# Stick-breaking attention: the second head's multiply moves from VectorE to GpSimd, with a third tail buffer

## The chip, the cores and the metric

The kernel runs on one core of a Trainium2 chip. The metric is the device time of one execution in microseconds, median of the runs. The engines are TensorE (PE in the profile, PEld for its weight loads), VectorE (DVE), ScalarE (ACT), GpSimd (POOL) and SyncE (SP), which issues most DMAs. They run their instruction streams in order and independently of each other, and meet at semaphores.

## The reference, cut to what matters

The model is a two-layer decoder over 512 tokens of width 1024. Layer 0 mixes with RWKV-7 and sparse attention, layer 1 with stick-breaking attention; behind each stands a mixture of 32 experts. The change lies in layer 1's attention alone, 16 heads of 64:

```python
def one_block(args):
    blk, qb = args
    q_pos = blk * Q_BLOCK + jnp.arange(Q_BLOCK)
    z = jnp.einsum('bqhd,bshd->bhqs', qb, k).astype(jnp.float32) * HEAD_DIM ** -0.5
    before = key_pos[None, :] < q_pos[:, None]
    log_keep = jnp.where(before, jax.nn.log_sigmoid(-z), 0.0)
    log_tail = lax.cumsum(log_keep, axis=3, reverse=True) - log_keep
    weight = jnp.where(before, jnp.exp(jax.nn.log_sigmoid(z) + log_tail), 0.0)
    return jnp.einsum('bhqs,bshd->bqhd', weight.astype(v.dtype), v)
```

A query gives each earlier key the share sigmoid(z) of what the keys between that key and the query have left over: the product of 1 - sigmoid(z) over these keys. That product is called the tail here.

## The kernel before, in words

The program is a row of stages, each closed by a barrier of all engines: constants, the even mixer (projection, preparation, RWKV chunks, sparse attention), experts, the odd mixer (projection `odd_project`, then `stick_breaking`), the output projection with the router, experts, final norm. The change touches `stick_breaking` (from L1083) only. While that stage runs, the only DMAs are the two loads of the output projection's weights at its start.

The work is cut into 32 units (t, f): a block t of 128 queries and a pair f of heads, t from 3 down to 0 and for each t the eight pairs. A unit sees L = (t + 1) * 128 keys, so there are eight units each of 512, 384, 256 and 128 keys, called the four quarters below. Tiles are 128 queries (partitions) by 2 heads by L keys. The order is written out by hand, one stream for each engine:

- TensorE, round i: `scores(i)` (L1114, two matmuls into the scores bank), `turn(i-2)` (L1124, transposes of the weights, one for each head and block of 128 keys, all heads of a unit in one go once `weighted` says so), `weigh(i-3)` (L1137, weights times v).
- ScalarE, round i: keep = sigmoid(-z) (L1167) and beta = sigmoid(z) (L1169) of unit i for both heads, then the copy of the transposed weights of unit i-2 out of PSUM (L1177), and every fourth time the output (L1155). It may run ahead until the four buffers of keep and beta are used up (`scanned`, `turned`).
- GpSimd, unit i: two affine_select masks (L1190) of the diagonal block, keep filled with 1 and beta with 0, 128 x 2 x 128 elements each, then `masked`.
- VectorE, unit i: waits for `masked`, then two scans (L1206), one for each head, that run backwards over the keys and form the running product of keep in `tail[i % 2]`; the third operand is the tile `zero`, added at each step. Then one multiply (L1210) over both heads, beta times tail shifted by one key, 2L elements, in place in beta, which sets `weighted`. Column T of tail holds 1.

For one unit of 512 keys the timeline thus shows two scans of 512, one multiply of 1024, two masks of 256, eight transposes, sixteen small matmuls and four score matmul instructions.

Outside the stage, three lines of `mixers_prepare` in layer 0 are spoken of because they show GpSimd's multiply beside VectorE's: L1617 (GpSimd, k_mod times inverse_W, 128x512) and L1679 (VectorE, rate times inverse_W, 128x512, both from SBUF).

Of the kernel before, what the change touches and what calls it, by code (L numbers as in the profile page):

```python
# [22 lines left out]
ALU = mybir.AluOpType  # L23
# [3 lines left out]
P = 128  # L27
BANK = 512
D = 1024
T = 512  # L30
# [1050 lines left out]
@stage  # L1081
def stick_breaking(nc, c, ctx, ps, qT, kT, v, yT, w_out, wts):

    PAIRS = C_HEADS // 2
    units = [(t, f) for t in reversed(range(TT)) for f in range(PAIRS)]
    N = len(units)
    DEEP, LAG_T, LAG_PV = 4, 2, 3
    keep = [c.sb(f"keep{i}", [P, 2, T], ctx=ctx) for i in range(DEEP)]
    beta = [c.sb(f"beta{i}", [P, 2, T], ctx=ctx) for i in range(DEEP)]
    tail = [c.sb(f"tail{i}", [P, 2, T + 1], ctx=ctx) for i in range(2)]  # L1090
    wT = [c.sb(f"wT{i}", [P, 2, T], ctx=ctx) for i in range(2)]
    zero = c.sb("zero", [P, T], ctx=ctx)
    z_done, beta_done, masked = c.sem("z_done"), c.sem("beta_done"), c.sem("masked")
    scanned, weighted = c.sem("scanned"), c.sem("weighted")
    turned, wT_out, pv_done, y_out, ready = (c.sem("turned"), c.sem("wT_out"), c.sem("pv_done"),
                                             c.sem("y_out"), c.sem("stick_ready"))
    two = lambda i: c.psum[:, i:i + 2, :]
    ps_z, ps_t, ps_y = [two(0), two(2)], two(4), [ps[6], ps[7]]

    with nc.Block() as block:  # L1100

        @block.sync
        def _(sp):
            wts.load_guest(sp, w_out)

        @block.tensor
        def _(pe):
            def scores(u):
                t, f = units[u]
                if u >= 2:  # L1110
                    pe.wait_ge(beta_done, 2 * (u - 2) + 2)
                for a in range(2):
                    q = slice(a * HD, (a + 1) * HD)
                    nc.tensor.matmul(ps_z[u % 2][:, a, 0:(t + 1) * P], qT[q, f, t * P:(t + 1) * P],  # L1114
                                     kT[q, f, 0:(t + 1) * P], start=True, stop=True).then_inc(z_done, 1)

            def turn(u):
                t, f = units[u]
                pe.wait_ge(weighted, u + 1)
                if u >= 1:  # L1120
                    pe.wait_ge(wT_out, u)
                for a in range(2):
                    for b in range(t + 1):
                        last = nc.tensor.transpose(ps_t[:, a, b * P:(b + 1) * P],  # L1124
                                                   beta[u % DEEP][:, a, b * P:(b + 1) * P], c.ident[:, :])
                last.then_inc(turned, 1)

            def weigh(u):
                t, f = units[u]
                half = u // 4  # L1130
                pe.wait_ge(wT_out, u + 1)
                if u % 4 == 0 and half >= 2:
                    pe.wait_ge(y_out, half - 1)
                for b in range(t + 1):
                    for a in range(2):
                        h = 2 * f + a
                        last = nc.tensor.matmul(ps_y[half % 2][a * HD:(a + 1) * HD, (f % 4) * P:(f % 4 + 1) * P],  # L1137
                                                v[:, b, h * HD:(h + 1) * HD], wT[u % 2][:, a, b * P:(b + 1) * P],
                                                start=b == 0, stop=b == t)
                last.then_inc(pv_done, 1)  # L1140

            for i in range(N + LAG_PV):
                if i < N:
                    scores(i)
                if 0 <= i - LAG_T < N:
                    turn(i - LAG_T)
                if 0 <= i - LAG_PV < N:
                    weigh(i - LAG_PV)

        @block.scalar  # L1150
        def _(act):
            def empty(half):
                t, f = units[4 * half]
                act.wait_ge(pv_done, 4 * half + 4)
                nc.scalar.activation(yT[:, f:f + 4, t * P:(t + 1) * P],  # L1155
                                     ps_y[half % 2][:, :].rearrange("p (f n) -> p f n", f=4),
                                     ACT.Copy).then_inc(y_out, 1)

            for i in range(N + LAG_T):
                if i < N:  # L1160
                    t, f = units[i]
                    L = (t + 1) * P
                    act.wait_ge(z_done, 2 * i + 2)
                    if i >= DEEP:
                        act.wait_ge(scanned, 2 * (i - DEEP + 1))
                        act.wait_ge(turned, i - DEEP + 1)
                    nc.scalar.activation(keep[i % DEEP][:, :, 0:L], ps_z[i % 2][:, :, 0:L], ACT.Sigmoid,  # L1167
                                         scale=-1.0).then_inc(beta_done, 1)
                    nc.scalar.activation(beta[i % DEEP][:, :, 0:L], ps_z[i % 2][:, :, 0:L],  # L1169
                                         ACT.Sigmoid).then_inc(beta_done, 1)  # L1170
                u = i - LAG_T
                if u >= 0:
                    L = (units[u][0] + 1) * P
                    act.wait_ge(turned, u + 1)
                    if u >= 2:
                        act.wait_ge(pv_done, u - 1)
                    nc.scalar.activation(wT[u % 2][:, :, 0:L], ps_t[:, :, 0:L], ACT.Copy).then_inc(wT_out, 1)  # L1177
                    if u % 4 == 2 and u > 4:
                        empty(u // 4 - 1)
            empty(N // 4 - 1)  # L1180

        @block.gpsimd
        def _(pool):
            for i, (t, f) in enumerate(units):
                pool.wait_ge(beta_done, 2 * i + 2)
                lo, hi = t * P, (t + 1) * P

                for buf, fill in ((keep, 1.0), (beta, 0.0)):
                    part = buf[i % DEEP][:, :, lo:hi]
                    last = nc.gpsimd.affine_select(out=part, in_=part, compare_op=ALU.is_gt, fill=fill, base=0,  # L1190
                                                   pattern=[[0, 2], [-1, P]], channel_multiplier=1)
                last.then_inc(masked, 1)

        @block.vector
        def _(dve):
            nc.vector.memset(zero[:, :], 0.0).then_inc(ready, 1)
            for i in range(2):
                nc.vector.memset(tail[i][:, :, T:T + 1], 1.0).then_inc(ready, 1)
            dve.wait_ge(ready, 3)
            for i, (t, f) in enumerate(units):  # L1200
                L = (t + 1) * P
                dve.wait_ge(masked, i + 1)
                if i >= 2:
                    dve.wait_ge(weighted, i - 1)
                for a in range(2):
                    nc.vector.tensor_tensor_scan(tail[i % 2][:, a, T - L:T][:, ::-1],  # L1206
                                                 keep[i % DEEP][:, a, 0:L][:, ::-1], zero[:, 0:L], 1.0,
                                                 ALU.mult, ALU.add).then_inc(scanned, 1)
                dve.wait_ge(scanned, 2 * i + 2)
                nc.vector.tensor_tensor(beta[i % DEEP][:, :, 0:L], beta[i % DEEP][:, :, 0:L],  # L1210
                                        tail[i % 2][:, :, T - L + 1:T + 1], ALU.mult).then_inc(weighted, 1)


def odd_mixer(nc, c, ps, x, gain, w_qkv, w_out, wts, slots, combine):
    ctx = c.ctx.enter_context(ExitStack())
    yT = c.sb("yT", [P, KD, T], ctx=ctx)
    with ExitStack() as inner:
        qT = c.sb("qT", [P, KD, T], ctx=inner)
        kT = c.sb("kT", [P, KD, T], ctx=inner)
        v = c.sb("v", [P, TT, D], ctx=inner)  # L1220
        with ExitStack() as proj:
            xn = c.sb("xn", [P, TT, D], ctx=proj)
            odd_project(nc, c, proj, ps, x, xn, gain, w_qkv, qT, kT, v, combine)
        wts.add_slot(slots, SLOTS - 1)
        stick_breaking(nc, c, inner, ps, qT, kT, v, yT, w_out, wts)
    for j in range(SLOTS - 1):
        wts.add_slot(slots, j)
    return yT, ctx
# [1112 lines left out]
```

## Time and profile before

| | us |
|---|---|
| median of 3 runs | 2202.16 |
| lowest and highest | 2191.27, 2206.74 |
| the profiled execution | 2199.79 |
| its span in the profile | 2198.1 |
| TensorE busy in the span | 1806.3 (82%) |
| VectorE busy | 686.5 (31%) |
| ScalarE busy | 426.0 (19%) |
| GpSimd busy | 175.5 (8%) |

The shares are averages over stages with different limits: the two expert stages take about half of the span and wait for TensorE and weights, so they say little of the attention stage. For a change in one stage, the views are to be read over that stage's stretch alone. In a line of the timeline, the bracket tells how long the engine was idle before and what it waited for; "x2" means that two instructions of the same line were merged, and the time is that of both.

### The profile page before, as it was taken

To read this page: it belongs to the slowest core of one execution; us is meant where nothing else is said; L and a number is where in the kernel's file an instruction comes from. 1 tells how busy PE (TensorE), PEld (TensorE's weight loads), DVE (VectorE), ACT (ScalarE), POOL (GpSimd) and SP (SyncE) were. 2 spreads that over 40 slices of the span, in tenths; PEclk is the share of its full clock that TensorE was granted. 3 is DMA by queue.
4 is the path that set the end of the run, shared out by engine and by line. 5 is a ranking of instruction groups with operands and counts; after the bars stand their busy time and mean duration, and the time that the engine had idled before them with its cause. 6 is when DMAs were issued, how large, how long until landed. Compare 5 with 4: busy or idle time off the path is not lost. (4 is left out here: it accounts for less than half of the span.)

```text
span 2198.1 us, 23093 instructions
## 1 busy us (share of the span) xinstructions
PE 1806.3 (82%) x8688; PEld 1002.6 (46%) x8817; DVE 686.5 (31%) x1146; ACT 426.0 (19%) x741; POOL 175.5 (8%) x207
## 2 busy tenths in 40 slices
PE   5999689999999598888887849978959888778883
PEld 4775288887554232323322237855423232223231
DVE  5532956556532211111111153358131111111113
ACT  4224322122321010000000031257111000000001
POOL 0000611221100100000000010035010000000001
PEclk9999779988569799998999959999979999888897
DMA  4300000001016599999999642120658999999993
GB/s 154 96 20 20 1 1 1 1 1 47 31 28 266 224 376 406 412 409 403 406 406 397 245 172 96 39 77 1 236 206 346 402 404 403 395 396 398 398 375 143
DMA packets 99115, 485.74 MB, mean 221 GB/s; under 512 B 30848, under 2 KB 55424, under 8 KB 74464
## 3 DMA queue, kind: packets, MB, share of 16 engines
q1 hardware_dynamic: 86112, 454.97, 53.1%
q0 software_dynamic: 4736, 17.17, 2.1%
q10 hardware_dynamic: 8192, 12.59, 1.7%
q8 instruction: 48, 0.79, 0.2%
q14 instruction: 27, 0.22, 0.0%
HBM read 461.24 MB, written 23.46 MB: 221 GB/s over the span
## 5 line engine op out<-in xcount | busy, mean ns | idle before, releaser
L558 PE MATMUL ps<-w,xT 128*48 128x512 f32 x1024 | 523.9, 671 | 160.7 <-DMA w<-in_moe_w 157.9
L559 PE MATMUL ps<-w,xT 128*48 128x512 f32 x1024 | 524.5, 672 | 0.0
L558 PEld LDWEIGHTS ps<-w,xT 128*48 128x48 f32 x1024 | 135.4, 137 | 528.5 <-issue 428.7
L582 DVE TENSOR_TENSOR xT<-ps,gain 128x384 f32<-128x384 f32 x64 | 35.7, 558 | 763.8 <-PE ps L551 763.8
L576 PE MATMUL ps<-w,hidT 128*48 128x512 f32 x512 | 234.3, 600 | 3.7 <-ACT hidT L599 3.7
L577 PE MATMUL ps<-w,hidT 128*48 128x512 f32 x512 | 234.2, 600 | 0.0
L997 PE MATMUL ps<-hT_high,w_high 128*128 128x512 f32 (+1 forms) x344 | 138.5, 403 | 30.0 <-DVE w_low L974 23.9
L599 ACT ACTIVATE hidT<-ps 128x192 f32<-128x192 f32 x64 | 21.2, 332 | 679.8 <-PE ps L567 677.5
L999 PE MATMUL ps<-hT_high,w_low 128*128 128x512 f32 (+1 forms) x344 | 136.6, 397 | 0.0
L998 PE MATMUL ps<-hT_low,w_high 128*128 128x512 f32 (+1 forms) x344 | 136.2, 396 | 0.0
L559 PEld LDWEIGHTS ps<-w,xT 128*48 128x48 f32 x1024 | 135.3, 137 | 0.0
L209 PE MATMUL ps<-w,yT 128*128 128x512 f32 x256 | 113.0, 604 | 3.1 <-PEq L76 3.1
L576 PEld LDWEIGHTS ps<-w,hidT 128*48 128x48 f32 x512 | 58.1, 123 | 123.6 <-issue 116.1
L595 DVE COPY y<-ps 48x512 f32<-48x512 f32 x64 | 44.4, 694 | 157.1 <-PE ps L577 157.1
L997 PEld LDWEIGHTS ps<-hT_high,w_high 128*128 128x128 f32 (+1 forms) x344 | 64.9, 189 | 53.2 <-ACT w_high L982 24.4
L609 ACT ACTIVATE y<-ps 48x512 f32<-48x512 f32 x64 | 37.9, 592 | 250.3 <-PE ps L577 250.3
L974 DVE TENSOR_TENSOR w_low<-w_raw,w_cut 128x2048 fp32r<-128x2048 f32 (+1 forms) x26 | 57.5, 2213 | 72.0 <-PEq L992 71.5
L209 PEld LDWEIGHTS ps<-w,yT 128*128 128x128 f32 x256 | 49.4, 194 | 65.5 <-issue 65.5
L999 PEld LDWEIGHTS ps<-hT_high,w_low 128*128 128x128 f32 (+1 forms) x344 | 64.6, 188 | 16.1
L998 PEld LDWEIGHTS ps<-hT_low,w_high 128*128 128x128 f32 (+1 forms) x344 | 64.9, 189 | 15.3
L551 PE MATMUL ps<-ident,x_rows 48*128 48x48 f32 x512 | 69.1, 275 | 2.6 <-DMA gain<-in_moe_norm 0.2
L551 PEld LDWEIGHTS ps<-ident,x_rows 48*128 48x128 f32 x512 | 61.2, 199 | 0.8
(338 smaller groups left out, 2458.5 us busy)
## 6 DMA issues: line engine op xcount, KB each, us to landing
w<-in_moe_w SPq DMA_DIRECT2D x192, 2048.0 KB, 26.9
x_rows<-sorted_rows SPq DMA_DIRECT2D x64, 192.0 KB, 24.8
expert_rows<-y ACTq DMA_DIRECT2D x128, 96.0 KB, 7.5
w_raw<-in_od_w_qkv SPq DMA_DIRECT2D x12, 1024.0 KB, 5.4
w_raw<-in_ev_w_in SPq DMA_DIRECT2D x10, 1024.0 KB, 5.4
w<-in_ev_w_out SPq DMA_DIRECT2D x2, 2048.0 KB, 11.8
w<-in_od_w_out SPq DMA_DIRECT2D x2, 2048.0 KB, 10.4
x<-in_x SPq DMA_DIRECT2D x4, 512.0 KB, 4.9
```

The lines of the kernel that those rows point to most:

```text
L209: last = self.nc.tensor.matmul(self.ps[2 * t + h][:, :], self.yT[:, f, t * P:(t + 1) * P], w[h][:, f, :], start=f == 0, stop=f == KD - 1)
L551: last = nc.tensor.transpose(ps_x[:, k * MB:(k + 1) * MB], x_rows[j][:, k::KD], c.ident[0:MB, 0:MB])
L558: nc.tensor.matmul(ps_1[b][0:MB, :], xT[b][:, k, :], w1_sb[j][:, k, :], start=k == 0, stop=k == KD - 1)
L559: last = nc.tensor.matmul(ps_3[b][UP:UP + MB, :], xT[b][:, k, :], w3_sb[j][:, k, :], start=k == 0, stop=k == KD - 1)
L576: nc.tensor.matmul(ps_y0[0:MB, :], hidT[:, k, :], w2_sb[j][:, k, 0:FF], start=k == 0, stop=k == KF - 1)
L577: last = nc.tensor.matmul(ps_y1[UP:UP + MB, :], hidT[:, k, :], w2_sb[j][:, k, FF:D], start=k == 0, stop=k == KF - 1)
L595: nc.vector.tensor_copy(y_sb[j][UP:UP + MB, :], ps_y1[UP:UP + MB, :]).then_inc(y1_out, 1)
L609: nc.scalar.activation(y_sb[j][0:MB, :], ps_y0[0:MB, :], ACT.Copy).then_inc(y0_out, 1)
L974: self.nc.vector.tensor_tensor(self.low[g % 2][:, :, 0:n], raw[:, :, 0:n], self.cut[:, :, 0:n], ALU.subtract).then_inc(self.low_done, 1)
L997: nc.tensor.matmul(out, lhsT[0], rhs[0], start=start, stop=False)
L998: nc.tensor.matmul(out, lhsT[0], rhs[1], start=False, stop=False)
L999: return nc.tensor.matmul(out, lhsT[1], rhs[0], start=False, stop=stop)
```

## The change

In the units of the attention, VectorE multiplies only the first head of each pair (L elements) and waits for the first scan alone; GpSimd multiplies the second head, one unit behind its masks: after the masks of unit i it waits for both scans of unit i-1 and multiplies that unit's second head, and after the last masks it does the last one. A new semaphore, `weighted_second`, tells TensorE that the second head is there; its wait stands between the transposes of the first head and those of the second. The tail buffers are three, and the scans of unit i wait for both multiplies of unit i-3.

```diff
-    tail = [c.sb(f"tail{i}", [P, 2, T + 1], ctx=ctx) for i in range(2)]
+    TAILS = 3
+    tail = [c.sb(f"tail{i}", [P, 2, T + 1], ctx=ctx) for i in range(TAILS)]
...
-    scanned, weighted = c.sem("scanned"), c.sem("weighted")
+    scanned, weighted, weighted_second = c.sem("scanned"), c.sem("weighted"), c.sem("weighted_second")
...
                 t, f = units[u]
-                pe.wait_ge(weighted, u + 1)
                 if u >= 1:
                     pe.wait_ge(wT_out, u)
                 for a in range(2):
+                    pe.wait_ge(weighted_second if a else weighted, u + 1)
                     for b in range(t + 1):
...
         def _(pool):
+            def second_head(u):
+                L = (units[u][0] + 1) * P
+                pool.wait_ge(scanned, 2 * u + 2)
+                part = beta[u % DEEP][:, 1, 0:L]
+                nc.gpsimd.tensor_tensor(part, part, tail[u % TAILS][:, 1, T - L + 1:T + 1],
+                                        ALU.mult).then_inc(weighted_second, 1)
+
             for i, (t, f) in enumerate(units):
...
                 last.then_inc(masked, 1)
+                if i >= 1:
+                    second_head(i - 1)
+            second_head(N - 1)
...
-            for i in range(2):
+            for i in range(TAILS):
                 nc.vector.memset(tail[i][:, :, T:T + 1], 1.0).then_inc(ready, 1)
-            dve.wait_ge(ready, 3)
+            dve.wait_ge(ready, 1 + TAILS)
             for i, (t, f) in enumerate(units):
                 L = (t + 1) * P
                 dve.wait_ge(masked, i + 1)
-                if i >= 2:
-                    dve.wait_ge(weighted, i - 1)
+                if i >= TAILS:
+                    dve.wait_ge(weighted, i - TAILS + 1)
+                    dve.wait_ge(weighted_second, i - TAILS + 1)
                 for a in range(2):
-                    nc.vector.tensor_tensor_scan(tail[i % 2][:, a, T - L:T][:, ::-1],
+                    nc.vector.tensor_tensor_scan(tail[i % TAILS][:, a, T - L:T][:, ::-1],
                                                  keep[i % DEEP][:, a, 0:L][:, ::-1], zero[:, 0:L], 1.0,
                                                  ALU.mult, ALU.add).then_inc(scanned, 1)
-                dve.wait_ge(scanned, 2 * i + 2)
-                nc.vector.tensor_tensor(beta[i % DEEP][:, :, 0:L], beta[i % DEEP][:, :, 0:L],
-                                        tail[i % 2][:, :, T - L + 1:T + 1], ALU.mult).then_inc(weighted, 1)
+                dve.wait_ge(scanned, 2 * i + 1)
+                nc.vector.tensor_tensor(beta[i % DEEP][:, 0, 0:L], beta[i % DEEP][:, 0, 0:L],
+                                        tail[i % TAILS][:, 0, T - L + 1:T + 1], ALU.mult).then_inc(weighted, 1)
```

GpSimd's instructions from the start of the stage, before. The names are tiles with a running number: keep_421 to keep_424 and beta_425 to beta_428 are the four buffers of each, so a pair of rows is one unit.

```order
L1190 AFFINE_SELECT keep_421<-keep_421 128x2x128
L1190 AFFINE_SELECT beta_425<-beta_425 128x2x128
L1190 AFFINE_SELECT keep_422<-keep_422 128x2x128
L1190 AFFINE_SELECT beta_426<-beta_426 128x2x128
L1190 AFFINE_SELECT keep_423<-keep_423 128x2x128
L1190 AFFINE_SELECT beta_427<-beta_427 128x2x128
```

The same place now; tail_429 to tail_431 are the three tail buffers.

```order
L1198 AFFINE_SELECT keep_421<-keep_421 128x2x128
L1198 AFFINE_SELECT beta_425<-beta_425 128x2x128
L1198 AFFINE_SELECT keep_422<-keep_422 128x2x128
L1198 AFFINE_SELECT beta_426<-beta_426 128x2x128
L1189 TENSOR_TENSOR beta_425<-beta_425,tail_429 128x512
L1198 AFFINE_SELECT keep_423<-keep_423 128x2x128
L1198 AFFINE_SELECT beta_427<-beta_427 128x2x128
L1189 TENSOR_TENSOR beta_426<-beta_426,tail_430 128x512
```

The multiply of a unit stands behind the masks of the next unit and ahead of those of the one after it; 32 such instructions are new on GpSimd.

VectorE's instructions from the start of the stage, before (the scan's rows bear the name of a three-operand operation here; keep0 and beta0 are the first of the four buffers).

```order
L1198 MEMSET tail1_430 128x2
L1206 SCALAR_TENSOR_TENSOR tail0_429<-keep0_421,zero_433 128x512 x2
L1210 TENSOR_TENSOR beta0_425<-beta0_425,tail0_429 128x1024
L1206 SCALAR_TENSOR_TENSOR tail1_430<-keep1_422,zero_433 128x512 x2
L1210 TENSOR_TENSOR beta1_426<-beta1_426,tail1_430 128x1024
```

The same place now.

```order
L1218 SCALAR_TENSOR_TENSOR tail0_429<-keep0_421,zero_434 128x512 x2
L1222 TENSOR_TENSOR beta0_425<-beta0_425,tail0_429 128x512
L1218 SCALAR_TENSOR_TENSOR tail1_430<-keep1_422,zero_434 128x512 x2
L1222 TENSOR_TENSOR beta1_426<-beta1_426,tail1_430 128x512
L1218 SCALAR_TENSOR_TENSOR tail2_431<-keep2_423,zero_434 128x512 x2
```

The order on VectorE stays; the multiply has half the elements, and the tail buffers go round over three.

## Rows read from the trace of the kernel before

**Rows 1.** The page's head.
```profile
span 2198.1 us, 23093 instructions
```

**Rows 2.** Table of stretches: the whole attention stage, and its last quarter.
```profile
core 0: us, PE busy (x) PEld busy (x) DVE busy (x) ACT busy (x) POOL busy (x), PEclk, DMA share, GB/s
1448.00:1541.20 93.20, 72.38 (x608) 45.11 (x608) 78.21 (x99) 67.52 (x105) 50.13 (x64) 0.96 0.13 46
...
1526.70:1541.20 14.50, 10.68 (x92) 6.24 (x92) 9.74 (x24) 8.83 (x24) 6.41 (x14) 0.96 0.01 2
```

**Rows 3.** Waits in the stage: who waited for whom, us in total, times, longest.
```profile
PEld ps L1124 <- DVE beta L1210: 33.0, 29, 4.5
...
DVE tail L1206 <- POOL beta L1190: 11.0, 20, 3.6
```

**Rows 4.** Groups by shape in the stage: VectorE's multiply, busy us, mean ns, idle before.
```profile
L1210 DVE TENSOR_TENSOR beta<-beta,tail 128x1024 f32<-128x1024 f32 x8 | 9.9, 1238 | 0.3
...
L1210 DVE TENSOR_TENSOR beta<-beta,tail 128x768 f32<-128x768 f32 x8 | 7.8, 974 | 0.3
...
L1210 DVE TENSOR_TENSOR beta<-beta,tail 128x512 f32<-128x512 f32 x8 | 5.6, 704 | 0.3
...
L1210 DVE TENSOR_TENSOR beta<-beta,tail 128x256 f32<-128x256 f32 x8 | 3.7, 468 | 0.3
```

**Rows 5.** Timeline of the first quarter: start us, us, engine, line, operation [idle before].
```profile
1451.84 0.40 POOL L1190 TENSOR_SCALAR_AFFINE_SELECT beta<-beta 128x256 f32<-128x256 f32 x1
...
1454.88 1.24 DVE L1210 TENSOR_TENSOR beta<-beta,tail 128x1024 f32<-128x1024 f32 x1
...
1456.05 2.69 DVE L1206 TENSOR_TENSOR_SCAN tail<-keep,zero 128x512 f32<-128x512 f32 x2
...
1468.09 2.34 DVE L1206 TENSOR_TENSOR_SCAN tail<-keep,zero 128x512 f32<-128x512 f32 x2 [0.30 <-POOL beta L1190]
...
1469.21 1.42 POOL L1190 TENSOR_SCALAR_AFFINE_SELECT keep<-keep 128x256 f32<-128x256 f32 x1 [1.16 <-ACT beta L1169]
...
1470.46 1.24 DVE L1210 TENSOR_TENSOR beta<-beta,tail 128x1024 f32<-128x1024 f32 x1
1470.58 1.39 POOL L1190 TENSOR_SCALAR_AFFINE_SELECT beta<-beta 128x256 f32<-128x256 f32 x1
...
1471.76 1.09 PE L1124 MATMUL ps<-ident,beta 128*128 128x128 f32 x8 [0.74 <-DVE beta L1210]
1472.00 2.34 DVE L1206 TENSOR_TENSOR_SCAN tail<-keep,zero 128x512 f32<-128x512 f32 x2 [0.30 <-POOL beta L1190]
...
1472.78 1.09 PE L1137 MATMUL ps<-wT,v 128*64 128x128 f32 x16
...
1473.81 1.13 PE L1114 MATMUL ps<-kT,qT 64*128 64x512 f32 x4
...
1475.01 1.02 ACT L1167 ACTIVATE keep<-ps 128x1024 f32<-128x1024 f32 x1 [1.06 <-PE ps L1114]
...
1475.93 1.02 ACT L1169 ACTIVATE beta<-ps 128x1024 f32<-128x1024 f32 x1
```

**Rows 6.** Timeline of layer 0's preparation: multiplies of both engines, alone and together.
```profile
232.64 0.69 DVE L1679 TENSOR_TENSOR rate<-rate,inverse_W 128x512 f32<-128x512 f32 x1
...
253.40 1.26 POOL L1617 TENSOR_TENSOR k_mod<-k_mod,inverse_W 128x512 f32<-128x512 f32 x1 [4.52 <-DVEq L1677]
253.41 1.80 DVE L1679 TENSOR_TENSOR rate<-rate,inverse_W 128x512 f32<-128x512 f32 x1
...
264.98 1.80 DVE L1679 TENSOR_TENSOR rate<-rate,inverse_W 128x512 f32<-128x512 f32 x1
```

## The prediction, made before the changed kernel ran

> **What bounds the kernel now.** I read the page's first line for the span, then the table of stretches for the one stage that the change touches, then that stage's waits, its groups by shape, and last the timeline of one unit. The stage of stick-breaking attention lies between 1448.0 and 1541.2 us: 93.2 us of a span of 2198.1 us [rows 1, 2]. Nothing outside it is touched, and everything behind it waits for it, so what it gains or loses moves the end by the same amount. In it VectorE is busy 78.2 us, TensorE 72.4, ScalarE 67.5 and GpSimd 50.1 [rows 2]. The waits say who is late: the weight loads of the transposes (L1124) wait 33.0 us for VectorE's multiply, while VectorE's scans wait 11.0 us for GpSimd's masks, 3.6 of them at the stage's start [rows 3]. So VectorE sets the pace of the first three quarters; in the last one (heads against 128 keys) it is busy only 9.7 of 14.5 us [rows 2].
>
> The timeline shows one unit of the first quarter: two scans 2.34 us from 1468.09, the multiply 1.24 us from 1470.46, the end of the mask of beta at 1471.97 (1470.58 + 1.39), the next scans at 1472.00 [rows 5]. The unit takes 3.91 us. The reader is to see two more things here. A mask instruction takes 0.40 us when VectorE is idle (1451.84) but 1.42 and 1.39 us beside a scan or a multiply, and it ends 0.2 to 0.3 us after the VectorE instruction that it lay beside, whenever it began [rows 5]. So GpSimd does not compute beside these instructions, it waits for them. The second mask's rest, about 0.3 us, is the pause before the next scan.
>
> **The change, part by part.** (1) VectorE multiplies one head instead of two. The multiply of 1024, 768, 512 and 256 elements takes 1238, 974, 704 and 468 ns, eight of each [rows 4]; half of each is 704, 586 (the mean of its neighbours), 468 and, one more half step down, about 350 ns. The saving is 0.53, 0.39, 0.24 and 0.12 us per unit, times eight 10.2 us in all, all of it on the engine that sets the pace.
>
> (2) GpSimd gets 32 multiplies of 512 to 128 elements. The same operation at 128x512 takes it 1.26 us with nothing beside it that hinders it (L1617 at 253.40) [rows 6]. If it ran beside VectorE, it would cost nothing, as GpSimd is free for 43 us of the stage. It does not. VectorE's multiply of two SBUF tiles of 512 elements takes 0.69 us alone (232.64), but 1.80 us where such a GpSimd multiply began 0.01 us before it, both times that this happened (253.41 and 264.98) [rows 6]. GpSimd's multiply therefore holds VectorE up for 1.80 - 0.69 = 1.11 us. Scans read two SBUF tiles too (keep and zero), and the masks show that they shut GpSimd out. For the shorter multiplies no row of before has a price; I take it in proportion to the elements: 1.11, 0.83, 0.55 and 0.28 us, times eight 22.2 us. (If it came at no price at all it is the first rival; the whole 1.26 us instead of 1.11 would make it 25.2.)
>
> The Trainium skill, "SBUF — State Buffer", section "Who interferes with whom", says that an instruction of VectorE with two SBUF inputs and a GpSimd instruction that reads SBUF shut each other out for the whole instruction, and that the one issued first goes first. By the trace the hold-up is 1.11 us, a little less than the whole 1.26; by that rule the added term would be 25.2 us and the result 3 us later than mine. The same skill's "Perfetto Trace Analysis", section "Optimizing Scalar/DVE Operations", warns that moving work between these two engines might not help for that reason.
>
> (3) The first head's multiply waits for the first scan only, and not for the second. Now the scans end at 1470.43 and the multiply begins at 1470.46, 0.03 us later; where nothing has to be waited for, VectorE's instructions overlap by 0.07 us (the multiply from 1454.88 ends at 1456.12, the next scan begins at 1456.05) [rows 5]. That is worth at most 0.10 us in each of 32 units, 3.2 us; but a mask uses the same gap now, and would push VectorE elsewhere. I take 1 us of it, with 0 and 3.2 as the bounds.
>
> (4) GpSimd masks unit i and then multiplies unit i-1. The masks of unit i+1 stand behind the multiply of unit i-1, and that one behind the wait for the scores of unit i; TensorE's second half of the transposes waits for it, then the weighing and the next scores behind them. The masks come later by the multiply's 1.26 us, but the pace of the whole is slower too. VectorE's waits for the masks, 11.0 - 3.6 = 7.4 us, can shrink, as ScalarE now has more time in each unit, but not by the part in which the mask itself is worked. I take 1 us less, bounds 0 and 7.4.
>
> (5) The third tail buffer: a scan waits for the multiplies three units back instead of two. The multiply that frees the buffer was on VectorE itself, just done; on GpSimd the multiply of unit i-3 stands ahead of the masks of unit i, for which the scans of unit i wait anyway, so the added wait is never the last. Worth nothing either way. The extra memset is one of two elements before the first scan, hidden in VectorE's 3.6 us wait at the start. The additional semaphore waits of TensorE and VectorE stand where the awaited event is either the bound itself or long past.
>
> Sum: +22.2 - 10.2 - 1 - 1 = +10 us. Checked against one unit of the first quarter: 3.91 - 0.53 + 1.11 = 4.49 us. The bounds of this case are 22.2 - 10.2 - 3.2 - 7.4 = +1.4 and 25.2 - 10.2 = +15 us. The profiled execution took 2199.8 us, so it would take 2209.8; the median of the runs shown is 2.4 us above it, which gives 2212. I forecast 2211 us.
>
> **Rival 1, faster: the two multiplies lie beside each other.** If the hold-up seen at 253.41 does not come up here, because GpSimd's multiply finds room in the pauses of VectorE, the 10.2 us are saved and the next limit decides. It is a loop over two units: GpSimd's multiply of unit u, half of the transposes (0.55), the weighing (1.09), the next scores (1.13), two activations (about 1.95), two masks (0.8), and GpSimd's multiply of unit u+2 (1.26), 6.8 us and some 0.3 of handing over, 3.55 us per unit instead of 3.91 [rows 5, 6]. That is 0.36 us in each of the first eight units, in proportion 7 us over all four quarters: 2202.2 - 7 = 2195 us. For it speaks that TensorE and ScalarE have room; against it the two rows of 1.80 us and the masks of 1.39 us.
>
> **Rival 2, slower by over 1%: the order in GpSimd's queue.** The same loop with GpSimd shut out at each step: masks of 1.42 and 1.39 us instead of 0.8, the multiply 1.26 plus a scan of 1.17 ahead of it. It is then 0.55 + 1.09 + 1.13 + 1.95 + 2.8 + 2.4 + 0.5 = 10.4 us for two units, 5.2 per unit against 3.91: 1.3 us more in the first quarter's units, and in proportion to 1, 3/4, 1/2, 1/4 over all 32 units 8 x 1.3 x 2.5 = +26 us, 2228 us. It decides from the point at which half the loop is longer than VectorE's own 4.49 us. For it speaks that GpSimd would be busy nearly throughout; against it that not every step of the loop meets the worst case.
>
> **Rival 3: nothing measurable,** since the hold-ups fall mostly into VectorE's pauses: its 11.0 us of waits and the last quarter's 4.8 us of idle time. Then hold-up and saving cancel: 2202 us.
>
> **How the numbers follow.** The forecast's case has 0.58, rival 1 0.15, rival 2 0.15, rival 3 0.12. The lower end takes in most of rival 1 (2196), the upper end most of rival 2 (2226). A measurement of this kernel can tell about 1%, 22 us, from no change. A gain of over 1% would need more than the 10.2 us that VectorE can save, so it is left with 0.02; a loss of over 1% is rival 2 for the most part, 0.13; within 1% is 0.85.
>
> **What would show it.** Right: the stage grows from 93 to about 103 us; scans next to a GpSimd multiply rise from 1.2 to some 2.3 us at 512 elements; VectorE's busy time in the stage goes up although its work went down; TensorE's wait is split between VectorE and GpSimd. Rival 1: scans stay at 1.2 us, GpSimd's multiplies at 1.3. Rival 2: VectorE's scans wait for GpSimd's masks by far more than 11 us. The prediction is wrong if the stage is under 95 or over 109 us.

## The result, and the profile after

| | before | after | |
|---|---|---|---|
| median of 20 runs each, us | 2193.02 | 2205.48 | ratio 1.0055, 95% interval 1.004 to 1.007 |
| lowest, highest | 2186.77, 2206.74 | 2198.73, 2215.66 | |
| profiled execution, us | 2199.79 | 2205.2 | |
| its span | 2198.1 | 2203.5 | +5.4 |
| the attention stage in it | 92.6 | 98.1 | +5.5 |

The forecast was 2211 us in a range from 2196 to 2226, and the measured time lies 5.5 us below it, well inside the range. The ratio and the profile do not tell the same size, though: 12.5 us between the medians, 5.4 us between the profiled spans, all of it in the attention stage. That gap is taken up behind the experiments; until then the stage alone is read.

Head of the page after, and the table of stretches over the stage (answers to [rows 1, 2]; the stage before is 92.6 us long when its window is drawn as tightly as this one):

```profile
span 2203.5 us, 23125 instructions
```

```profile
core 0: us, PE busy (x) PEld busy (x) DVE busy (x) ACT busy (x) POOL busy (x), PEclk, DMA share, GB/s
...
1447.70:1545.90 98.20, 78.68 (x608) 45.28 (x608) 85.22 (x100) 68.56 (x105) 73.48 (x96) 0.95 0.12 44
```

VectorE has fewer elements to work through and is busy 7.0 us longer (85.2 against 78.2). GpSimd is busy 23 us longer. The waits of the stage (answer to [rows 3]; who waited for whom, us, times, longest):

```profile
PEld ps L1125 <- POOL beta L1189: 15.1, 30, 0.8
DVE tail L1218 <- POOL beta L1198: 10.1, 19, 3.6
...
PE ps L1125 <- DVE beta L1222: 8.7, 15, 3.2
PE ps L1125 <- POOL beta L1189: 8.0, 22, 0.6
```

TensorE's transposes now wait for GpSimd as well as for VectorE, in turns. The groups by shape (answer to [rows 4]; busy us, mean ns):

```profile
L1218 DVE TENSOR_TENSOR_SCAN tail<-keep,zero 128x512 f32<-128x512 f32 x16 | 25.9, 1657 | 4.2 <-POOL beta L1198 4.2
...
L1218 DVE TENSOR_TENSOR_SCAN tail<-keep,zero 128x384 f32<-128x384 f32 x16 | 20.6, 1324 | 1.2 <-POOL beta L1198 1.2
...
L1218 DVE TENSOR_TENSOR_SCAN tail<-keep,zero 128x256 f32<-128x256 f32 x16 | 14.2, 924 | 2.2 <-POOL beta L1198 2.2
L1189 POOL TENSOR_TENSOR beta<-beta,tail 128x512 f32<-128x512 f32 x8 | 11.3, 1413 | 0.0
...
L1218 DVE TENSOR_TENSOR_SCAN tail<-keep,zero 128x128 f32<-128x128 f32 x16 | 8.0, 536 | 2.5 <-POOL beta L1198 2.5
L1222 DVE TENSOR_TENSOR beta<-beta,tail 128x512 f32<-128x512 f32 x8 | 6.6, 823 | 0.0
```

The scans are the kernel's untouched part, and they are what grew. Before they took:

```profile
L1206 DVE TENSOR_TENSOR_SCAN tail<-keep,zero 128x512 f32<-128x512 f32 x16 | 19.4, 1253 | 5.4 <-POOL beta L1190 5.4
...
L1206 DVE TENSOR_TENSOR_SCAN tail<-keep,zero 128x384 f32<-128x384 f32 x16 | 14.9, 972 | 1.9 <-POOL beta L1190 1.9
L1206 DVE TENSOR_TENSOR_SCAN tail<-keep,zero 128x256 f32<-128x256 f32 x16 | 10.9, 722 | 1.9 <-POOL beta L1190 1.9
...
L1206 DVE TENSOR_TENSOR_SCAN tail<-keep,zero 128x128 f32<-128x128 f32 x16 | 6.4, 438 | 1.9 <-POOL beta L1190 1.9
```

From 1253 to 1657, 972 to 1324, 722 to 924 and 438 to 536 ns, sixteen of each: 6.5 + 5.6 + 3.2 + 1.6 = 16.9 us. The timeline after (answer to [rows 5]) shows where:

```profile
1463.43 1.09 POOL L1189 TENSOR_TENSOR beta<-beta,tail 128x512 f32<-128x512 f32 x1
1463.50 3.22 DVE L1218 TENSOR_TENSOR_SCAN tail<-keep,zero 128x512 f32<-128x512 f32 x2 [0.30 <-POOL beta L1198]
...
1467.77 3.38 DVE L1218 TENSOR_TENSOR_SCAN tail<-keep,zero 128x512 f32<-128x512 f32 x2 [0.30 <-POOL beta L1198]
...
1471.07 0.82 DVE L1222 TENSOR_TENSOR beta<-beta,tail 128x512 f32<-128x512 f32 x1
1471.32 1.52 POOL L1189 TENSOR_TENSOR beta<-beta,tail 128x512 f32<-128x512 f32 x1
...
1471.82 3.41 DVE L1218 TENSOR_TENSOR_SCAN tail<-keep,zero 128x512 f32<-128x512 f32 x2
...
1473.74 0.41 POOL L1198 TENSOR_SCALAR_AFFINE_SELECT keep<-keep 128x256 f32<-128x256 f32 x1 [0.90 <-ACT beta L1170]
...
1474.10 1.33 POOL L1198 TENSOR_SCALAR_AFFINE_SELECT beta<-beta 128x256 f32<-128x256 f32 x1
...
1475.15 0.82 DVE L1222 TENSOR_TENSOR beta<-beta,tail 128x512 f32<-128x512 f32 x1
```

GpSimd's multiply is asked for at 1471.32, while VectorE multiplies; it gets its turn behind that and ends at 1472.84. VectorE's pair of scans, which took 2.34 us before, begins at 1471.82 and takes 3.41. The unit takes 1475.15 - 1471.07 = 4.08 us instead of 3.91. In the rows at the top GpSimd's multiply came 0.07 us before the scans and was held up by nobody; then it takes 1.09 us and the scans wait, and that unit takes 1467.77 - 1463.50 = 4.27 us.

A row "x2" and a mean over sixteen hide which scan waits. The scans one by one (shortest, median, longest, ns; the kernel before, then the changed one):

```profile
L1206 DVE TENSOR_TENSOR_SCAN tail<-keep,zero x64: 392/926/1418, 1452.3 to 1537.8; 128x512 f32<-128x512 f32 x16, 128x384 f32<-128x384 f32 x16, 128x256 f32<-128x256 f32 x16, 128x128 f32<-128x128 f32 x16
```

```profile
L1218 DVE TENSOR_TENSOR_SCAN tail<-keep,zero x64: 391/1104/2109, 1452.0 to 1542.6; 128x512 f32<-128x512 f32 x16, 128x384 f32<-128x384 f32 x16, 128x256 f32<-128x256 f32 x16, 128x128 f32<-128x128 f32 x16
```

In the changed kernel's trace it is the first scan of a pair that takes 2.11 us at 512 elements; the second takes 1.19 to 1.38. The mean of 1.66 is that of both kinds.

### The profile page after: what moved, and what is told of

Its sections match the earlier page's. It is cut to its first block and busy times, and to the rows that moved or that the text cites. A ratio compares the mean times of both kernels' runs of the same rounds, so it can differ in the third digit from the quotient of the medians.

```text
span 2203.5 us, 23125 instructions
## 1 busy us (share of the span) xinstructions
PE 1811.4 (82%) x8688; PEld 1001.7 (45%) x8817; DVE 693.4 (31%) x1147; ACT 427.2 (19%) x741; POOL 200.4 (9%) x239
## 5 line engine op out<-in xcount | busy, mean ns | idle before, releaser
L1218 DVE TENSOR_TENSOR_SCAN tail<-keep,zero 128x512 f32<-128x512 f32 (+3 forms) x64 | 68.6, 1110 | 10.1 <-POOL beta L1198 10.1
## 6 DMA issues: line engine op xcount, KB each, us to landing
w<-in_od_w_out SPq DMA_DIRECT2D x2, 2048.0 KB, 10.3
```

The costliest lines, as they stand in the source:

```text
L1218: nc.vector.tensor_tensor_scan(tail[i % TAILS][:, a, T - L:T][:, ::-1], keep[i % DEEP][:, a, 0:L][:, ::-1], zero[:, 0:L], 1.0, ALU.mult, A ...
```

## The experiments

"Stage" is the attention stage from its first instruction to the last one that writes its output, in each run's profile; before it is 92.6 us. Each total has its ratio to the kernel before on the same chip.

**1. The buffer alone.** Three tail buffers, and the scans' wait moved by one unit:

```diff
-                if i >= 2:
-                    dve.wait_ge(weighted, i - 1)
+                if i >= 3:
+                    dve.wait_ge(weighted, i - 2)
```

> The kernel before with three tail buffers and nothing else. The port theory (GpSimd's multiply and VectorE's instructions shut each other out) expects no effect of the buffer: the attention stage stays at 92.5 to 93 us, total within 0.2% of before. The rival that the buffer or its wait costs or brings something expects the stage to move by over 1 us.

Measured: stage 92.4 us, ratio 1.0001 (0.9977 to 1.0025). The third buffer does nothing by itself.

**2. The saving alone.**

```diff
-                nc.vector.tensor_tensor(beta[i % DEEP][:, :, 0:L], beta[i % DEEP][:, :, 0:L],
-                                        tail[i % 2][:, :, T - L + 1:T + 1], ALU.mult).then_inc(weighted, 1)
+                nc.vector.tensor_tensor(beta[i % DEEP][:, 0, 0:L], beta[i % DEEP][:, 0, 0:L],
+                                        tail[i % 2][:, 0, T - L + 1:T + 1], ALU.mult).then_inc(weighted, 1)
```

> The kernel before, in which VectorE multiplies the first head only and nobody the second (the second head's weights stay unmultiplied): the saving alone. By halves of the multiply's groups VectorE has 10.2 us less work; I expect the stage at 84 to 88 us, since masks and ScalarE then hold VectorE up in part. If the saving comes out at under 4 us, the change could not have gained even with a free second multiply, and my term for the saving was the wrong one.

Measured: stage 84.1 us, 8.5 less than before. VectorE is busy 67.1 us in it instead of 78.2, 11.1 less, and its waits for the masks grow from 11.0 to 13.7 us. The total (2461.5 us) says nothing: other numbers reach the router, and the expert stage behind it alone takes 778 us instead of 522.

**3. The hold-up without the saving.** GpSimd multiplies into a scratch tile, one unit behind its masks as in the change. TensorE doesn't wait for it; VectorE's scans do, three units later:

```diff
+                nc.gpsimd.tensor_tensor(scratch[:, 0:L], tail[u % 3][:, 1, T - L + 1:T + 1], zero[:, 0:L],
+                                        ALU.mult).then_inc(spare, 1)
```

> The kernel before with three tails, and beside it a GpSimd multiply of the second tail with zero into a scratch tile behind each unit's masks, of the same sizes as in the change; TensorE does not wait for it, VectorE still does the whole multiply. It is the hold-up alone. The port theory expects scans or multiplies of VectorE longer by about 1.0 us a unit at 512 elements and 16 to 17 us in all (as the changed kernel's scans are), less 3 us of pauses that vanish: the stage at 104 to 109 us. The rival that the loss came from TensorE's wait for GpSimd expects the stage to stay under 96 us.

Measured: stage 106.1 us, 13.5 more, ratio 1.008 (1.0054 to 1.0106). The stretch of the stage, the scans' group and that of GpSimd's new instruction:

```profile
1445.40:1551.60 106.20, 77.88 (x608) 48.87 (x608) 96.24 (x100) 68.09 (x105) 89.47 (x96) 0.90 0.11 40
```

```profile
L1220 DVE TENSOR_TENSOR_SCAN tail<-keep,zero 128x512 f32<-128x512 f32 x16 | 25.9, 1655 | 4.2 <-POOL beta L1200 4.2
...
L1191 POOL TENSOR_TENSOR scratch<-tail,zero 128x512 f32<-128x512 f32 x8 | 14.5, 1812 | 0.0
```

The scans are at 1655 ns, as in the changed kernel, although TensorE waits for nothing that GpSimd multiplies. The rival of TensorE's wait (under 96 us) is out. VectorE is busy 18.0 us longer than before (96.2 against 78.2), and 4.5 us of that come out of its pauses. The saving of run 2 and the 13.5 us of this one give 92.6 - 8.5 + 13.5 = 97.6 us, and the changed kernel has 98.1. That the sum fits so closely is in part luck: neither run has the earlier start of the first head's multiply, which gains something (run 5), nor TensorE's wait for GpSimd.

**4. Is it the reading?** GpSimd fills a scratch tile at the place of the multiply; the second head stays unmultiplied.

```diff
-                nc.gpsimd.tensor_tensor(part, part, tail[u % TAILS][:, 1, T - L + 1:T + 1],
-                                        ALU.mult).then_inc(weighted_second, 1)
+                n = 64 + L * 9 // 4
+                nc.gpsimd.memset(scratch[:, 0:n], 0.0).then_inc(weighted_second, 1)
```

> The changed kernel, in which GpSimd does not multiply the second head (its weights stay unmultiplied) but fills a scratch tile of 64 + 2.25 L elements at the same place in its queue and with the same semaphore: an instruction of about the same duration (1.1 us at 512) that writes SBUF and reads nothing. Time is read in the attention stage alone. The port theory, if it is the reading that shuts VectorE out, expects scans back at 1.2 us and the stage at 84 to 88 us. The rival of GpSimd's queue order and TensorE's wait expects it to stay at 95 us or more. If any GpSimd access to SBUF shuts VectorE out, it stays at 98.

Measured: stage 89.0 us (one timing; the total of 2458.4 us says as little as in run 2). That is between the two theories, and both ranges missed it. The scans' group, and two units' starts in the timeline:

```profile
L1220 DVE TENSOR_TENSOR_SCAN tail<-keep,zero 128x512 f32<-128x512 f32 x16 | 19.0, 1230 | 7.6 <-POOL beta L1200 7.6
```

```profile
1462.39 1.10 POOL L1192 MEMSET scratch<- 128x1216 f32 x1
1462.48 2.34 DVE L1220 TENSOR_TENSOR_SCAN tail<-keep,zero 128x512 f32<-128x512 f32 x2 [0.66 <-POOL beta L1200]
...
1465.97 1.11 POOL L1192 MEMSET scratch<- 128x1216 f32 x1
1466.06 2.34 DVE L1220 TENSOR_TENSOR_SCAN tail<-keep,zero 128x512 f32<-128x512 f32 x2 [0.66 <-POOL beta L1200]
```

An instruction of 1.10 us that only writes lies wholly beside the scans, and they take 2.34 us as if it weren't there. So it is GpSimd's reading of SBUF that shuts VectorE's two-input instructions out, and not its writing or the time that it is busy; that is worth 98.1 - 89.0 = 9.1 us. That a fill does not contend is what the Trainium skill, "SBUF — State Buffer", section "Who interferes with whom", states, and here the trace agrees. The order in GpSimd's queue costs too, though less than the rival said (95 us or more): 89.0 - 84.1 = 4.9 us above run 2. No run tells the queue order from TensorE's wait for GpSimd in this; the two come together here. The pace of 1466.06 - 1462.48 = 3.58 us per unit agrees with the loop through GpSimd's queue in the prediction's rival 1 (3.55 us).

**5. The cut alone.** Both heads on VectorE, one instruction for each, the first waiting for the first scan alone.

```diff
+                for a in range(2):
+                    dve.wait_ge(scanned, 2 * i + 1 + a)
+                    nc.vector.tensor_tensor(beta[i % DEEP][:, a, 0:L], beta[i % DEEP][:, a, 0:L],
+                                            tail[i % 3][:, a, T - L + 1:T + 1], ALU.mult).then_inc(weighted, 1)
```

> The kernel before with three tails, VectorE's multiply cut into one for each head, the first waiting for the first scan alone, TensorE waiting for each by itself. It tells the fixed price of two smaller multiplies and what the earlier first one brings. From halves of the groups the fixed part is 0.17 us (2 x 704 - 1238 ns) in 32 units, 5.4 us, less up to 3 us of pauses: the stage at 93 to 97 us. If it came out at 98, the loss of the change would lie in the cut and not in GpSimd.

Measured (one timing, 2187.7 us): stage 90.3 us, 2.3 less than before, where I had expected 93 to 97. The loss is not in the cut; the cut gains, and what moves the second head to GpSimd costs 98.1 - 90.3 = 7.8 us. The waits tell why:

```profile
1450.30:1540.70 90.40, 76.66 (x608) 45.31 (x608) 82.93 (x132) 67.01 (x105) 43.33 (x64) 0.95 0.13 48
```

```profile
L1206 DVE TENSOR_TENSOR_SCAN tail<-keep,zero 128x512 f32<-128x512 f32 x16 | 19.2, 1237 | 3.6 <-POOL beta L1190 3.6
...
L1206 DVE TENSOR_TENSOR_SCAN tail<-keep,zero 128x384 f32<-128x384 f32 x16 | 14.7, 956 | 0.0
```

The scans' waits for the second mask fell from 11.0 us to 3.6 + 0.0 + 0.3 + 1.0 (the two smaller shapes), of which 3.6 is the stage's start: GpSimd's mask now finds its gap between the two multiplies, and is done when the scans are due, as one unit shows (the mask ends at 1473.20, the scans begin at 1473.67):

```profile
1472.12 1.63 DVE L1211 TENSOR_TENSOR beta<-beta,tail 128x512 f32<-128x512 f32 x2
1472.35 0.85 POOL L1190 TENSOR_SCALAR_AFFINE_SELECT beta<-beta 128x256 f32<-128x256 f32 x1
...
1473.67 2.33 DVE L1206 TENSOR_TENSOR_SCAN tail<-keep,zero 128x512 f32<-128x512 f32 x2
```

The changed kernel against this run says where its 7.8 us are. The scans take 68.7 us instead of 50.6, 18.1 more, and VectorE's multiplies 19.6 instead of 36.6, 17.0 less: the hold-up eats up what VectorE is spared. VectorE, whose instructions overlap less often now, is busy 2.3 us longer in all (85.2 against 82.9), and the other 5.5 us are idle time, nearly all of it the waits for the masks (10.1 against 4.9 us), which now stand behind a multiply in GpSimd's queue.

**6. A version without the multiply.** Since keep is 1 - beta, beta times the shifted tail is the shifted tail less the tail; the sigmoid and the mask of beta go.

```diff
-                nc.vector.tensor_tensor(beta[i % DEEP][:, :, 0:L], beta[i % DEEP][:, :, 0:L],
-                                        tail[i % 2][:, :, T - L + 1:T + 1], ALU.mult).then_inc(weighted, 1)
+                nc.vector.tensor_tensor(beta[i % DEEP][:, :, 0:L], tail[i % 2][:, :, T - L + 1:T + 1],
+                                        tail[i % 2][:, :, T - L:T], ALU.subtract).then_inc(weighted, 1)
...
-            for buf, fill in ((keep, 1.0), (beta, 0.0)):
+            for buf, fill in ((keep, 1.0),):
```

> A version for both: beta times the tail ahead of it is that tail less the next one, since keep is 1 - beta; so VectorE takes the difference of two views of the tail in place of the multiply, and the sigmoid and the mask of beta go. VectorE's own work is the same. If VectorE and what GpSimd reads beside it set the pace, the second mask's 0.3 us pause and its place between scans go, 6 to 8 us in the stage: 84 to 87 us, total 0.3% faster. If the pace came from ScalarE or TensorE, more or less would go; if only VectorE's work counts, the stage stays within 2 us of 92.5.

Measured: stage 82.7 us, 9.9 less than before and somewhat under the expected 84; ratio 0.9972 (0.9944 to 1.0001). VectorE has the same instructions and sizes. What went is one mask of two and 18 us of ScalarE's work (67.5 to 49.7 us busy). VectorE's waits for GpSimd fell from 11.0 to 3.7 us, and it is busy 2.6 us less (78.2 to 75.6), so the 9.9 us are on VectorE's own account; what the lighter ScalarE gave to the shorter waits was not told apart from the missing mask.

**7. The same, cut on VectorE**, as in run 5, with three tails:

> The difference of tails in place of the multiply, and cut on VectorE into one instruction for each head as in the run with the cut multiply, with three tails. The cut gave 2.2 us there by removing the pause between scans and multiply and the wait for the second mask; the second mask is gone here already, so only the pause is left to gain, against 0.17 us of fixed price in each of 32 units. I expect the stage at 82 to 85 us, next to the 82.7 of the uncut difference, and the total 0.3 to 0.5% under before.

Measured: stage 82.3 us, as good as run 6; median 2173.06 against 2194.23 us, ratio 0.9892 (0.9855 to 0.9928). It is the fastest of all versions here. The stage's 10.3 us are sure. The total is 1.1% lower where I had expected 0.3 to 0.5%, and what makes up the rest of the 21 us between the medians is open: the interval leaves out 10.3 us (0.47%), and in the profiles the last expert stage, from its first matmul to its last, takes 505 to 509 us in the three versions with the difference of tails, 511 and 512 in runs 5 and 9, and 521 to 524 in the other versions that compute the full result.

**8. The same, with the second head's difference on GpSimd:**

```diff
+                nc.gpsimd.tensor_tensor(beta[u % DEEP][:, 1, 0:L], tail[u % 3][:, 1, T - L + 1:T + 1],
+                                        tail[u % 3][:, 1, T - L:T], ALU.subtract).then_inc(weighted_second, 1)
```

> The difference of tails with the second head's on GpSimd, one unit behind its mask, as in the change. The port theory expects the same price as there: 7 to 8 us more than the version cut on VectorE, the stage at 89 to 92 us, with scans at 1.6 us of 512 elements. The rival that the masks' queue was the larger part of the loss expects under 87 us, since only one mask is left in that queue.

Measured: stage 86.7 us, 4.4 more than run 7; ratio 0.9926 (0.9889 to 0.9962). Moving the second head costs here too, but less than the 7 to 8 us that I expected; the number is on the rival's side (under 87). The stretches of run 7 and of this run:

```profile
1446.10:1528.40 82.30, 72.62 (x608) 44.37 (x608) 77.25 (x132) 49.86 (x73) 22.93 (x32) 0.98 0.14 52
```

```profile
1437.70:1524.40 86.70, 76.14 (x608) 44.17 (x608) 80.46 (x100) 49.75 (x73) 52.75 (x64) 0.98 0.14 50
```

The scans are held up much as before (1652 ns by the mean of the sixteen at 512), and VectorE is busy 3.2 us longer than in run 7, next to 2.3 in the same comparison for the change. Its waits for the mask are only 3.8 us against 2.9, where the change had 10.1 against 4.9. So with one mask in GpSimd's queue instead of two the hold-up still eats up what VectorE is spared, but the idle time behind it is mostly gone.

**9. The rest of the gap: a pure delay, and the changed kernel twice more.** Three fills of 5.5 us in all behind the last output of the kernel before:

```diff
+            pool.wait_ge(y_out, N // 4)
+            for n in range(3):
+                nc.gpsimd.memset(idle[:, :], 0.0).then_inc(idled, 1)
+                pool.wait_ge(idled, n + 1)
```

> The kernel before, with three GpSimd fills of about 1.8 us one after the other behind the last output of the attention stage: 5.5 us of pure delay at its end, as much as the change costs there. If what follows the stage is only shifted, the total is 5 to 6 us over before (0.25%), less than the spread of a few runs. If a delay there is made larger by the expert stage behind it, the total is 10 us or more over before.

> The changed kernel once more, for its time beside the others on the same chip and a second profile. The stage's span is the same within 0.3 us (98.2 us, 5.5 more than before). The measured medians are 12.5 us apart, so 7 us are to be found elsewhere: if they are real, this run is 10 to 15 us over before and its stretches behind the attention stage are longer than those of before; if they are the spread of the expert stages, the gap here is anything from 3 to 15 us.

> The changed kernel a third time. Its stage costs 5.3 to 5.5 us more than before in both traces so far, yet the medians were 12.5 us apart once and 2 us once. If the rest is the spread of the DMA-bound expert stages, the gap here lies between 2 and 12 us again and the stage stays at 98 us; if the first gap was the true one, it is 10 us or more.

| run | stage, us | ratio of the totals, 95% interval | medians apart, us |
|---|---|---|---|
| after, first comparison | 98.1 | 1.0055 (1.004 to 1.007) | +12.5 |
| after, again | 97.9 | 1.0008 (0.9981 to 1.0035) | +2.0 |
| after, third | 98.0 | 0.9995 (0.9965 to 1.0024) | -1.0 |
| delay only (fills included) | 98.0 | 1.0053 (1.0024 to 1.0081) | +10.8 |

The stage costs 5.3 to 5.5 us each time; the totals scatter by more than that around it, and both repeats came out under the ranges that I had set. The intervals of the first comparison and the third do not even meet, so an interval tells how far the executions within one comparison scatter, and not how far comparisons do. The delay's interval holds its 5.5 us (0.25%) only at its lower edge, and it alone would have spoken for an enlargement; the changed kernel's second and third comparison speak against one. Why the first comparison gave 12.5 us stays open. The profiles show a part of the scatter in a place which no version touches. The stretch is that from 280 to 302 us, in the first chunk of layer 0's recurrence; the changed kernel's first profile and its third (the granted clock is the number behind the five engines):

```profile
280.00:302.00 22.00, 21.01 (x101) 20.41 (x100) 8.00 (x12) 1.36 (x4) 4.55 (x4) 0.50 0.00 1
```

```profile
280.00:302.00 22.00, 21.01 (x175) 20.52 (x174) 12.28 (x21) 5.76 (x11) 4.55 (x4) 0.92 0.00 1
```

The same program gets through 101 matmul records in one and 175 in the other. VectorE takes the products out of PSUM as TensorE delivers them, in the kernel before (clock 0.50) 1.71 us apart and in run 1 0.89 us apart:

```profile
286.25 0.69 DVE L2029 TENSOR_TENSOR QbT<-ps,mask 128x512 f32<-128x512 f32 x1 [1.01 <-PE ps L1907]
287.96 0.69 DVE L2029 TENSOR_TENSOR NT<-ps,mask 128x512 f32<-128x512 f32 x1 [1.01 <-PE ps L1907]
```

```profile
287.83 0.69 DVE L2029 TENSOR_TENSOR QbT<-ps,mask 128x512 f32<-128x512 f32 x1 [0.20 <-PE ps L1907]
288.72 0.69 DVE L2029 TENSOR_TENSOR NT<-ps,mask 128x512 f32<-128x512 f32 x1 [0.20 <-PE ps L1907]
```

Behind the stretch the changed kernel's first profile is 9.0 us later than its third (VectorE's L2075 begins at 338.92 against 329.92 us), and 7.4 us later one chunk further on (398.42 against 390.99). The attention stage began between 1435 and 1452 us in all profiles, and part of that is this one stretch. The expert stage behind it took 522 us before and 524, 522 and 521 in the three profiles of the changed kernel: the spread that I had looked for there is not in it.

## Why the prediction was right, point by point

**The bound and the place.** VectorE set the pace of the stage, and everything gained or lost in it moved the end; nothing outside changed by design. This held.

**(1) The saving, 10.2 us.** Run 2 gives 8.5 us where nothing else is added: 11.1 us less of VectorE's time, and 2.7 us more of waits for the masks (in 27 units against 20). In the changed kernel the multiplies' busy time fell from 27.0 to 19.6 us, by 7.4: at 512 elements 823 ns instead of the 704 taken. There a mask stands ahead of them (the one from 1470.03 us ends at 1471.35, inside the multiply from 1471.07). Where none does, as in run 4, the same multiply takes 0.67 us:

```profile
1464.73 0.67 DVE L1224 TENSOR_TENSOR beta<-beta,tail 128x512 f32<-128x512 f32 x1
```

**(2) The hold-up, 22.2 us.** The mechanism is shown: the changed kernel and run 4 differ in whether GpSimd's added instruction reads SBUF, and the scans are at 1657 or 1230 ns. The size was too large. The scans grew by 16.9 us, and 10.2 - 7.4 = 2.8 us fell on the multiplies, 19.7 us together, 2.5 less than forecast. The price from the rows of layer 0 (1.11 us at 512 elements) was too high for this stage. The longest scan is 2.11 us here against 1.20 to 1.23 for one that nothing holds up, so a multiply costs a scan 0.9 us; the trace has 1.61, 1.12 and 0.63 us at 384, 256 and 128 elements, which is 0.67, 0.44 and 0.21 more than without. The pair that takes 3.41 - 2.34 = 1.07 us longer also has a mask (from 1473.74) ahead of its second scan; the pair of 3.22 us has none there and is 0.88 longer. GpSimd's multiply takes only 1.09 us here when it is not held up itself (at 1463.43), not 1.26, and both in layer 0 and here VectorE loses 0.15 to 0.2 us less than that duration.

**(3) and (4) The pauses, 1 and 1 us.** Here the sizes were too small: 4.0 us. Fewer elements and more hold-up give 19.7 - 10.2 = 9.5 us more of VectorE's time, but the stage grew by 5.5 us. VectorE's busy time, in which instructions that overlap count once, grew by 7.0 us only; the 2.5 us between are term (3), within its bounds of 0 and 3.2. Its idle time went from 14.4 to 12.9 us, which is 1.5 us for term (4). The unit above shows it: scans +1.07, multiply -0.42, the 0.30 us wait for the second mask turned into an overlap of 0.07 (-0.37), the gap of 0.03 ahead of the multiply into an overlap of 0.08 (-0.11), in sum +0.17 us, 3.91 to 4.08. I had seen both pauses and took 2 us of the 10.6 that their bounds allow. Run 5 shows that the cut brings a gain without GpSimd: 2.3 us net of the higher fixed price of two instructions.

**(5) The third buffer, nothing:** run 1, 92.4 us.

**Sum.** Predicted +10 us in the stage, measured +5.5: term (2) was 2.5 us too large, and (3) and (4) 2.0 too small. That the median came so near to 2211 us is luck. The forecast stood on the 2202.2 us of three executions, and the median of twenty is 9 us lower; the first comparison then lay 12.5 us over that, of which the stage explains 5.5.

**The signs.** The stage is 98.1 us, short of the 103 named and over the 95 below which the prediction would have been wrong. A scan next to a GpSimd multiply rose to 2.11 us where 2.3 was named, VectorE's busy time went up by 7.0 us with less work, and TensorE's waits are split between VectorE and GpSimd. All the signs came, two of them smaller.

**The rivals.** Rival 1 (no hold-up, 3.55 us per unit by the loop) is what run 4 did when the reading was taken away: 3.58 us. Rival 2 (the loop with each step shut out, 5.2 us) did not come: the worst units take 4.27 us (scans at 1463.50 and 1467.77). Rival 3 (hold-up and saving cancel, as the pauses take them up) was nearer than its 0.12 suggested: of 9.5 us the pauses took up 4.0, and by the totals of the second and third comparison alone nothing measurable is what one would have seen.

## What to carry to other kernels

Before moving an elementwise instruction from VectorE to GpSimd, look in the trace for any place where the two have read SBUF at the same time: if the later of the two takes longer by nearly the other's duration, they take turns, and most of what the move takes off the path comes back as hold-up. Then look at what stands behind the moved instruction in the new engine's queue: here 5.5 of the 7.8 us lost against run 5 were idle time of VectorE, which waited for masks there. Where an engine sets the pace, look at the pauses of 0.03 to 0.3 us ahead of each of its instructions: cutting one instruction in two, each with its own wait, gained 2.3 us here, and a version without the mask on which the longest pause hung, and without the sigmoid ahead of it, gained 9.9.

## What the runs showed of the hardware that I had not expected

- A multiply of two SBUF tiles on GpSimd has two durations when nothing of VectorE is in its way: 1.26 us at 128x512 in layer 0 (253.40) and 1.09 in this stage. What it costs VectorE differs in the same way, 1.11 and 0.9 us. What sets it is open.
- The scan, too, takes turns with GpSimd's reads: 1.23 us at 512 elements beside a fill, 2.11 with a multiply ahead of it.
- A mask that gets its turn ahead of an instruction of VectorE costs it about 0.15 us (a multiply of 0.82 instead of 0.67 us), far less than the mask's own 0.40 us.
- In layer 0's recurrence the granted clock of TensorE is 0.50 from 280 to 302 us in one execution of the changed kernel and 0.80 and 0.92 in the two others: the lower level, 1.2 GHz, throughout, or 2.4 GHz for most of the stretch. Behind it the first and the third lie 7 to 9 us apart. TensorE is busy for 21.0 of the 22 us in both of the profiles shown, and what decides between them is open. A change of 5 us in this kernel can be read from its stage's span, which repeats within 0.2 us, and hardly from the totals of twelve runs.
